# A hybrid attention block: the first modulation in two column parts of 5 and 3 k-tiles

## What is computed

```
c_act = silu(c)
mod = c_act @ w_ada + b_ada                      # w_ada 1024 x 6144
sh1, sc1, gt1, sh2, sc2, gt2 = split(mod, 6)
h = rmsnorm(x, g_norm1) * (1 + sc1) + sh1
a_q, a_kv, i_q, i_k, i_w, b_q, ... = split(h @ w_in)   # w_in 1024 x 8136
score = sum_h i_w[h] * relu(i_q[h] . i_k)        # indexer, top 128 keys of each query
... three attention branches, gates, output projection, SwiGLU, final rmsnorm
```

## Time and profile before

| | us |
|---|---|
| median of 3 runs | 1054.0 (1052.38 to 1056.43) |
| the profiled execution | 1055.12 |
| its span in the trace | 1053.0 |
| PE busy | 1000.0 (95%) |
| first projection matmul starts | 44.82 |
| tile 4 starts | 69.38 |
| tile 6 starts | 81.96 |

### The profile page before, as it was taken

One profiled execution on the slowest core, in us unless ns is written; L12 is line 12 of the kernel. 1 busy time (PEld: TensorE's weight loads), 2 busy tenths in 40 slices (PEclk: granted clock), 3 DMA queues, 4 the chain that ended last, 5 costly groups with the idle time before them and its releaser, 6 DMA issues.

```text
span 1053.0 us, 12662 instructions
## 1 busy us (share of the span) xinstructions
PE 1000.0 (95%) x4831; PEld 809.4 (77%) x4831; DVE 484.5 (46%) x803; ACT 412.4 (39%) x676; POOL 115.7 (11%) x136
## 2 busy tenths in 40 slices
PE   2799999999999999999999999799999999999997
PEld 0677988878877766778888888588888888788886
DVE  3845687833235344553746567623233232322331
ACT  4434523255455655642222222433344433412231
POOL 3000000000044411200000026300000000001111
PEclk9799999999999999999999999899999999999999
DMA  8693134312130201155556583032322323223302
GB/s 305 223 295 119 51 116 139 113 48 81 61 102 21 72 21 31 34 177 175 169 176 211 197 282 115 3 120 80 120 80 81 118 84 115 70 80 110 110 31 80
DMA packets 93262, 121.49 MB, mean 115 GB/s; under 512 B 4680, under 2 KB 83109, under 8 KB 93090
## 3 DMA queue, kind: packets, MB, share of 16 engines
q1 hardware_dynamic: 92690, 114.67, 33.0%
q0 software_dynamic: 528, 6.22, 2.0%
HBM read 118.20 MB, written 8.45 MB: 120 GB/s over the span
## 4 chain that ended last, share of the span: by engine, by line
PE 86%; DMA 4%; DVE 4%; ACT 2%; SPq 2%; issue 1%; POOL 0%; POOLq 0%; DVEq 0%; ACTq 0%
PE tile_ps L762 24%; PE tile_ps L764 23%; PE tile_ps L763 23%; DMA w_raw<-in_w_in_dram 4%; PE s_ps L902 2%; PE t_ps L920 2%; PE o_ps L949 2%; SPq L517 2%; DVE w_lo L1438 1%; ACT w_hi L1143 1%; PE s_ps L905 1%; PE tile_ps L963 1%; PE tile_ps L1008 1%; PE tile_ps L969 1%; PE tile_ps L1009 1%
## 5 line engine op out<-in xcount | busy, mean ns | idle before, releaser
L762 PE MATMUL tile_ps<-h_hi,w_hi 128*128 128x512 f32 x816 | 326.9, 401 | 13.1 <-DVE h_lo L1845 4.3
L764 PE MATMUL tile_ps<-h_hi,w_lo 128*128 128x512 f32 x816 | 320.3, 393 | 0.0
L763 PE MATMUL tile_ps<-h_lo,w_hi 128*128 128x512 f32 x816 | 319.9, 392 | 0.0
L1438 DVE TENSOR_TENSOR w_lo<-w_raw,w_hi 128x2048 fp32r<-128x2048 f32 (+2 forms) x78 | 172.3, 2209 | 249.0 <-ACT w_hi L1143 249.0
L762 PEld LDWEIGHTS tile_ps<-h_hi,w_hi 128*128 128x128 f32 x816 | 153.9, 189 | 58.2 <-issue 16.7
L764 PEld LDWEIGHTS tile_ps<-h_hi,w_lo 128*128 128x128 f32 x816 | 153.9, 189 | 33.5
L1143 ACT ACTIVATE w_hi<-w_raw 128x2048 fp32r<-128x2048 f32 (+2 forms) x78 | 143.8, 1844 | 89.9 <-PE tile_ps L764 68.7
L763 PEld LDWEIGHTS tile_ps<-h_lo,w_hi 128*128 128x128 f32 x816 | 154.3, 189 | 29.9
L762 PE MATMUL tile_ps<-f_hi,w_hi 128*128 128x512 f32 x176 | 69.1, 393 | 2.5 <-DVE f_lo L1862 2.5
L764 PE MATMUL tile_ps<-f_hi,w_lo 128*128 128x512 f32 x176 | 69.2, 393 | 0.0
L763 PE MATMUL tile_ps<-f_lo,w_hi 128*128 128x512 f32 x176 | 69.1, 393 | 0.0
(11 more groups left out here) (272 smaller groups left out, 1354.1 us busy)
## 6 DMA issues: line engine op xcount, KB each, us to landing
w_raw<-in_w_in_dram SPq DMA_DIRECT2D x31, 1024.0 KB, 5.5
w_raw<-in_w_gate_up_dram SPq DMA_DIRECT2D x22, 1024.0 KB, 5.1
ada<-in_w_ada_dram SPq DMA_DIRECT2D x16, 1024.0 KB, 5.7
ada<-in_w_ada_dram SPq DMA_DIRECT2D x16, 512.0 KB, 15.4
w_raw<-in_w_down_dram SPq DMA_DIRECT2D x8, 1024.0 KB, 5.2
row_copies<-row_flat POOLq DMA_DIRECT2D x1, 5632.0 KB, 21.2
...
```

Source lines behind the costliest of these rows:

```text
L762: pe.matmul(tile_ps[b][0:mw, :], wh, x_hi[:, kx, :], start=start, stop=False)
L763: pe.matmul(tile_ps[b][0:mw, :], wh, x_lo[:, kx, :], start=False, stop=False)
L764: mm = pe.matmul(tile_ps[b][0:mw, :], wl, x_hi[:, kx, :], start=False, stop=stop)
L1438: dve.tensor_tensor(w_lo[s][:, 0:kt, :], w_raw[s][:, 0:kt, :], w_hi[s][:, 0:kt, :].bitcast(F32), ALU.subtract) \
```

## The change

- The 2048 columns of w_ada are summed in two parts. Part 0 has the columns of k-tiles 0 to 4 of both groups (8 blocks 128x2x640, 640 KB, rows of 2560 bytes), part 1 those of k-tiles 5 to 7 (8 blocks 128x2x384, rows of 1536 bytes). Chunk 0 is loaded behind the sixth block of part 0, chunk 1 behind the eighth, and part 1 behind that.
- Block 0 of part 0 isn't summed by DVE: PE multiplies it by c_act into PSUM in 10 matmuls 128x1, ahead of the transposes. The rest is added by 10 matmuls (`mod_part(0)`), part 1 by 6.
- x comes in four DMAs. ACT scales two of its blocks, DVE the other two.
- h_hi is made by ACT from x_T with scale and bias, no longer by a copy of h. The full h goes to four buffers h_full: k-tiles 0, 1, 5, 6, 7 by POOL, 2, 3, 4 by ACT. h_lo of 2, 3, 4 is subtracted by POOL, the rest by DVE.
- The four query tiles have four PSUM banks. PE runs the first five k-tiles of tiles 0, 1, 2, then `mod_part(1)`, the first five of tile 3, then the last three of tiles 0, 1, 2, 3.
- POOL issues the five small broadcasts behind the power of x's statistic. `row_copies` waits for the fifth h_lo of DVE, the last of all.

```diff
-        for g in range(2):
+        for q, kts in enumerate(FIRST_KTS):           # (range(0, 5), range(5, 8))
             for k in range(KT):
-                sp.dma_start(ada1[g][k][:], a["w_ada"][0][k * P:(k + 1) * P, g * D:(g + 1) * D]) \
+                sp.dma_start(ada1[q][k][:], w_ada[k * P:(k + 1) * P, 0:2, kts[0] * P:(kts[-1] + 1) * P]) \
+                if (q, k) in ((0, 5), (0, 7)):
+                    load(k // 7, ...)
...
+            power(1, rs_x, ms_x, 4)
             for j, n in enumerate(("lam_q1", "lam_k1", "lam_q2", "lam_k2")):
                 pool.dma_start(lamv[:, j, :], a[n].to_broadcast([P, DH])).then_inc(small_in, 16)
             pool.dma_start(gkv[:], a["g_kv"].to_broadcast([P, P])).then_inc(small_in, 16)
...
+            hidden_full(0)
+            hidden_full(1)
+            for kt in (2, 3, 4):
+                pool.wait_ge(h_full_act, kt - 1)
+                pool.wait_ge(h_hi_made, kt + 1)
+                pool.tensor_tensor(h_lo[:, kt, :], h_full[kt % 4][:], h_hi[:, kt, :].bitcast(F32), ALU.subtract)
+            for kt in FIRST_KTS[1]:
+                hidden_full(kt)
             pool.wait_ge(rows_stored, 16 * 4)
-            pool.wait_ge(h_ready, KT)
+            pool.wait_ge(h_ready, 5)
             pool.dma_start(rep_dram, row_dram.to_broadcast([P, FL_W])).then_inc(rows_copied, 16)
...
-            for g in range(2):
-                pe.wait_ge(ada1_added, KT * (g + 1))
-                mod_columns(ada1_sum[g], 8, 8 * g)
-            project_two(0, 0, ready=h_ready)
-            project_two(1, 2)
+            mod_part(0)
+            chunk_ready(0)
+            for t in range(2):
+                query_part(t, FIRST_KTS[0])
+            chunk_ready(1)
+            query_part(2, FIRST_KTS[0])
+            mod_part(1)
+            query_part(3, FIRST_KTS[0])
+            for t in range(4):
+                query_part(t, FIRST_KTS[1])
             project_two(2, 4, mw=(P, 72))
...
             make_hi(0, None)
-            for kt in range(KT):
-                act.wait_ge(h_full_made, kt + 1)
-                act.activation(h_hi[:, kt, :], x_T[:, kt, :], ACT.Copy).then_inc(h_hi_made, 1)
-            make_hi(1, None)
+            act.wait_ge(amp_ready, 1)
+            for kt in FIRST_KTS[0]:
+                hidden_hi(kt)
+                if kt >= 2:
+                    act.activation(h_full[kt % 4][:], x_T[:, kt, :], ACT.Identity, bias=..., scale=...)
+                if kt == 1:
+                    make_hi(1, None)
+            act.wait_ge(amp_ready, 2)
+            for kt in FIRST_KTS[1]:
+                hidden_hi(kt)
...
+            add_part(0, range(1, KT))
             make_lo(0)
-            dve.wait_ge(mod_made, 2)
...
+            amplitude(0)
+            hidden_lo(0, 1)
+            hidden_lo(1, 2)
+            add_part(1, range(0, 2))
             make_lo(1)
+            add_part(1, range(2, KT))
+            amplitude(1)
+            for n, kt in enumerate(FIRST_KTS[1]):
+                hidden_lo(kt, 3 + n)
```

More of the change, by code:

```diff
@@ L63 @@
 N_STEP = 88
+FIRST_KTS = (range(0, 5), range(5, 8))
 STEP_OC = 49
@@ L590, in load_ada2 @@
                 if j < 2:
[L591 removed]
+                    if n:
+                        sp.wait_ge(mod_made, n)
                 else:
@@ L792, in _, with turn_x @@
                           start=True, stop=True).then_inc(pe0, 1)
+            pe.wait_ge(ada1_in[0][0], 16)
+            pe.wait_ge(cols_ready, 2)
+            for g in range(2):
+                for m in range(5):
+                    pe.matmul(mod_ps[:, 8 * g + m:8 * g + m + 1], ada1[0][0][:, g, m * P:(m + 1) * P], c_act[:, 0:1],
+                              start=g == 0 and m == 0, stop=False)
             pe.wait_ge(x_scaled, NBLK)
             pe.wait_ge(brow_out, 3)
-            for kt in range(KT):
+            def turn_x(kt):
                 if kt >= 4:
@@ L1160, in _ @@
                                accum_out=ms_x[:, b:b + 1]).then_inc(x_sq, 1)
-            act.wait_ge(pow_out, 1)
-            for b in range(NBLK):
-                act.activation(x_nat[:, b, :], x_nat[:, b, :], ACT.Copy, scale=rs_x[:, b:b + 1]).then_inc(x_scaled, 1)
             for j, ps in enumerate((t_ps[0], t_ps[1], s_ps[1])):
@@ L1465, in _ @@
-            make_lo(0)
-            dve.wait_ge(mod_made, 2)
-            link(dve.tensor_tensor(mod[:, 0:16], mod_ps[:, 0:16], b_ada[:, 0:16], ALU.add))
-            link(dve.scalar_tensor_tensor(out=amp1, in0=scale1, scalar=1.0, in1=g_n1, op0=ALU.add, op1=ALU.mult))
-            dve.wait_ge(xt_read, KT)
-            for kt in range(KT + 1):
-                if kt < KT:
-                    dve.tensor_scalar(x_T[:, kt, :], x_T[:, kt, :], amp1[:, kt:kt + 1], shift1[:, kt:kt + 1],
-                                      ALU.mult, ALU.add).then_inc(h_full_made, 1)
-                if kt:
-                    k = kt - 1
-                    dve.wait_ge(h_hi_made, k + 1)
-                    dve.tensor_tensor(h_lo[:, k, :], x_T[:, k, :], h_hi[:, k, :].bitcast(F32), ALU.subtract) \
-                        .then_inc(h_ready, 1)
+            dve.sem_inc(cols_ready, 1)
@@ new lines, in amplitude @@
+            def amplitude(q):
+                dve.wait_ge(mod1_made, q + 1)
+                k0, n = FIRST_KTS[q][0], len(FIRST_KTS[q])
+                for g in range(2):
+                    c0 = 8 * g + k0
+                    ins = dve.tensor_tensor(mod[:, c0:c0 + n], mod_ps[:, c0:c0 + n], b_ada[:, c0:c0 + n], ALU.add)
+                link(ins)
+                dve.scalar_tensor_tensor(out=amp1[:, k0:k0 + n], in0=scale1[:, k0:k0 + n], scalar=1.0,
+                                         in1=g_n1[:, k0:k0 + n], op0=ALU.add, op1=ALU.mult).then_inc(amp_ready, 1)
```

136 lines of the change are left out of this document (98 added, 38 removed).

## The result

| | before | after |
|---|---|---|
| median of 19 runs each, us | 1053.63 (1051.6 to 1058.48) | 1058.05 (1055.91 to 1059.64) |
| ratio to before, 95% interval | | 1.0037 (1.0028 to 1.0046) |
| the profiled execution, its span | 1055.12, 1053.0 | 1056.78, 1055.0 |
| amp1 ready (X) | 42.7 | 35.92 |
| first projection matmul | 44.82 | 37.74 |

The change makes the kernel 0.37% slower, about 3.9 us by the ratio of the runs (the medians stand 4.4 us apart), clear of the noise, though its first projection matmul starts 7 us earlier. The forecast was 1058.0. The sum is right at its end, but two of its terms were wrong by 1.3 and 1.6 us with opposite signs, and the experiments are mostly about these.

A forecast was written before the change was run, and what follows sets the result against it. PE, busy 1000 of 1053.0 us, was taken as the bound, leaving only its waits, nearly all before tile 6. Tile 6 starting 3.75 later gave 1058.9 profiled, 1057.8 against the median, so 1058; range 1053 to 1061.5.

The forecast's parts named there:

- Part 0 of the sum: Start of the kernel: last block of w_ada's first part lands at 30.5, amp1 ready at 37.2, 5.5 us earlier.
- moved and not saved: Small broadcasts at the start: their DMA loss of 2.6 us only moves into part 0's stream; 0.4 us taken as saved.
- Rival (2): Start of the kernel: broadcasts cost nothing in their new place, amp1 2.2 us earlier, kernel at 1055.6; chance 0.12.
- Turns: h_lo of k-tiles 2 to 4: DVE and POOL alternate whole instructions, k-tile 4 ready 12.1 us behind amp1, not 9.0.
- the row with 3.22: Profile row before the change: a POOL subtraction begun 0.2 us behind DVE's w_lo took 3.22 us, against 1.30 alone.
- Rival (1): h_lo subtractions: DVE and POOL don't hinder each other, k-tile 4 at amp1 + 9.0, kernel 3.5 us less, 1054.3; chance 0.17.
- The clock's rise and tile 1: PE in tiles 0 to 3: clock rises near 16 us behind amp1, tile 1 ends 30.45 behind it, at 67.65.
- Rival (3): PE in tiles 1 and 2: gaps keep the clock at 0.50, 4.7 us more, kernel at 1062.5; chance 0.13.
- What is late next: Before tile 4: 6.9 us of ACT and DVE work covered by 4.1, PE waits 2.8, tile 4 starts 5.2 later.
- the upper bound of X: Start of the kernel: the latest time allowed for amp1, 38.9, against a forecast of 37.2.

The follow-up runs named there:

- run 5: The five small broadcasts put back ahead of the power of x's statistic, against the kernel after; ratio to before 1.0043 (1.0028 to 1.0058).
- run 1: DVE holds back w_lo of chunk 1 and the rest of part 1's sum until POOL's three subtractions are done, against after; ratio to before 1.0008.
- run 3: PE ends tiles 0 and 1 before it goes on with tile 3, against the kernel after; ratio to before 1.0007 (0.9997 to 1.0018).
- runs 1 to 4: Four single edits of after: DVE held back, 1.0008 to before; DVE subtracts for POOL, 0.9997; other PE order, 1.0007; tiles 4 and 5 released earlier, 1.0005.

## Why the prediction was right

**Part 0 of the sum: mis-sized by 1.3 us.** Forecast: last block landed at 30.5, amp1 at 37.2. The last two blocks were added back to back from 27.75, so the last had landed by 29.4, and amp1 came at 35.92 (35.9 to 36.6 in ten traces). The term that failed is "moved and not saved", of which I took 0.4 us: the broadcasts cost about 1.1 us less in their new place by the DMA rates, 0.7 to 1.4 by the start of PE's small matmuls (run 5). Rival (2) was half true, and the rest lies within what one trace differs from the next; the landing of chunk 0 at 38.15, from which the sum counted back, was itself 0.9 us earlier in the second trace of before. The ten small matmuls took 4.43 (4.5 forecast), three steps to amp1 0.46 (0.55).

**Turns: right.** Three subtractions in 6.92 us, k-tile 4 at X + 11.8 (12.1 forecast), the first of them drawn out to 3.03 us behind w_lo, as the row with 3.22 had it. Rival (1), no turns, put it at X + 9.0, and with DVE held back it stood at 9.0. The Trainium skill, page "SBUF — State Buffer", section "Who interferes with whom", has DVE with two inputs in SBUF and POOL exclude each other; the 2.8 and 2.7 us that came off both sides in run 1 agree.

**The clock's rise and tile 1: right in this trace.** Rise at X + 14.7 (16 forecast), tile 1's end at X + 29.95 (30.45). In the second trace of after the rise came at X + 16.4. Rival (3), 0.50 all through tiles 1 and 2, came about in no trace of after.

**What is late next: right.** From the end of tile 1 to tile 4 7.05 us (6.9), a wait of 2.99 (2.8), caused by the late end of tile 1 (run 3). No wait at tile 6 and tile 8; chunk 4 was split from 88.2 on (90.3 forecast for its landing).

**What was missing.** Tile 4 to tile 6 was taken over from before as 11.15 us. It took 12.72, since the clock fell by half around tile 4. I had priced the wait of PE at its length; with the fall behind it it cost 4.6. The rows for that were at hand: the earlier trace rows show the clock at 0.50 within a wait of PE of only 2.70 us, and the sum used that for the ten small matmuls but not here. This 1.6 is cancelled by the 1.3 of part 0 and the 0.3 net of the two terms between: tile 6 at 85.67 (85.7 forecast).

**The total.** The trace's tile 6 is 3.71 later than before's, the ratio of the runs says 3.9, and the sum had 3.75. The two profiled spans differ by 2.0 only: of the 3.7, the fall of the clock at 397 in before alone took back 1.7. Had tile 6 been compared over the repeated traces (81.96 and 80.82; 85.67, 88.33 and 85.27), the shift would be 5.0, against 3.9 in the runs. That the size came out to the tenth is thus luck: two errors of opposite sign cancel in it. Sign and mechanism are shown: the edits of runs 1 to 4 each take back about 3 us or more of the 3.9. The range had two slips that the result didn't bring out: the upper bound of X, 38.9, leaves out the 0.4 us taken for the broadcasts (39.3), and the bounds given, added to 1057.8, make about 1054.7 to 1060, not 1055.5 to 1060.5. And 0.5% was too coarse a guess of what the runs can tell: 0.37% stood clear of an interval of 0.09% to each side.
